# The gate columns leave the front, and a new stage runs the first tile's merge and experts beside the other tiles' gates

## What is computed

```python
h = rmsnorm(x, norm1_w)
z = h @ w_in                       # columns: q, k, v (512 each), forget logits (8), GLU (1024), mq (512), gates (3072)
a = glu[:, :512] * sigmoid(glu[:, 512:])
gates = sigmoid(z[:, OFF_G:]).reshape(n, 3, 1024)
o_fox  = fox_attention(q, k, v, logf) @ w_fox_o
o_conv = silu(layernorm(causal_depthwise_conv31(a))) @ w_conv_o
o_mem  = memory_attention(mq, mk, mv) @ w_mem_o
x = x + (gates[0] * o_fox + gates[1] * o_conv + gates[2] * o_mem) @ w_out
h2 = rmsnorm(x, norm2_w)
# PEER: 8 heads; each picks 16 of 16384 experts for every row
q = (h2 @ w_q).reshape(n, 8, 2, 128)
s1, s2 = q[:, :, 0] @ keys1.T, q[:, :, 1] @ keys2.T        # 128 scores a side
top 16 of each side, top 16 of their 256 sums -> idx, g = softmax(top)
x = x + sum_k g[k] * gelu(h2 . u[idx[k]]) * v[idx[k]]      # u, v: 16384 rows of 1024
```

## Time and profile before

| | us |
|---|---|
| median of 3 runs | 4037.64 (4036.03 to 4041.02) |
| the profiled execution, from its first to its last instruction | 4041.3 |
| front, up to the barrier | 723 |
| attention, up to the barrier | 222 |
| merge of nine tiles | 230 |
| loop of 1088 steps | 2862 |

### The profile page before, as it was taken

How to read it: one execution, slowest core, us unless ns; L and a number is a source line. 1 busy time by engine, 2 the same in 40 slices (tenths; PEclk the granted TensorE clock), 3 DMA queues, 4 the chain that set the end, 5 groups by cost and what they waited for, 6 DMA issues and landing times.

```text
span 4041.3 us, 36528 instructions
## 1 busy us (share of the span) xinstructions
PE 3418.2 (85%) x10586; PEld 1797.4 (44%) x10586; DVE 2646.1 (65%) x6147; ACT 1002.9 (25%) x2536; POOL 2474.0 (61%) x2475
## 2 busy tenths in 40 slices
PE   8999999799988878877877887887888787788787
PEld 6788788455534333333333333333333333333332
DVE  4119944563476777777767777677777777767794
ACT  6111112673222212212222121221222212122131
POOL 4416531232037777777777777777677777777775
PEclk9989999899999999999999999999999999999999
DMA  4402234644279999999999999999999999999998
GB/s 154 129 27 91 99 101 135 168 124 166 84 279 409 409 409 410 409 409 409 402 404 410 407 399 409 405 401 409 405 400 409 408 397 406 409 389 399 409 406 313
DMA packets 419459, 1294.72 MB, mean 320 GB/s; under 512 B 62122, under 2 KB 98246, under 8 KB 419263
## 3 DMA queue, kind: packets, MB, share of 16 engines
q0 software_dynamic: 313344, 1140.99, 71.3%
q1 hardware_dynamic: 104554, 146.81, 11.5%
q10 hardware_dynamic: 1365, 4.60, 0.4%
HBM read 1247.62 MB, written 44.60 MB: 320 GB/s over the span
## 4 chain that ended last, share of the span: by engine, by line
DMA 34%; POOL 22%; PE 12%; issue 8%; DVE 1%; ACT 0%; SPq 0%; DVEq 0%; POOLq 0%
DMA late_v_rows<-in_peer_v,late_expert_idx 23%; POOL late_v_rows L1446 11%; POOL late_u_rows L1438 11%; DMA late_u_rows<-in_peer_u,late_expert_idx 8%; PE late_sums_ps L1635 5%; PE late_sums_ps L1486 4%; DMA late_u_rows<-in_peer_u,late_twin_idx 2%; PE late_q_ps L1526 1%; DMA late_v_rows<-in_peer_v,late_twin_idx 1%; DVE late_u_rows L1916 1%; PE late_h_T_ps L1508 1%; DMA late_w_q_high<-in_peer_w_q 1%; DMA gates<-scr_gates 0%; DMA scr_m<-merged 0%; PE late_rows_ps L1466 0%
## 5 line engine op out<-in xcount | busy, mean ns | idle before, releaser
L1635 PE MATMUL late_sums_ps<-late_v_rows,late_diag 128*128 128x512 f32 (+1 forms) x3840 | 1919.8, 629 | 545.3 <-DMA late_v_rows<-in_peer_v,late_expert_idx 503.5
L1916 DVE CUSTOM_DVE_ANT_0 late_u_rows<-late_u_rows,late_rows_ps 128x1024 f32<-128x1024 f32 x1072 | 1306.5, 1219 | 788.7 <-DMA late_u_rows<-in_peer_u,late_expert_idx 751.8
L1635 PEld LDWEIGHTS late_sums_ps<-late_v_rows,late_diag 128*128 128x128 f32 (+1 forms) x3840 | 682.3, 193 | 1644.3 <-issue 1591.8
L1446 POOL DMA_INDIRECT late_v_rows<-in_peer_v,late_expert_idx x1024 | 992.8, 970 | 404.2 <-issue 248.7
L1438 POOL DMA_INDIRECT late_u_rows<-in_peer_u,late_expert_idx x1008 | 969.6, 962 | 313.2 <-issue 290.5
L1709 ACT ACTIVATE late_gelu<-late_dots 128x4 f32<-128x4 f32 x272 | 55.7, 205 | 2133.1 <-DVE late_dots L1916 2133.1
L457 POOL CAST front_w_upper<-front_w_raw 128x512 fp32r<-128x512 f32 x110 | 107.7, 979 | 332.8 <-DMA front_w_raw<-in_w_in 285.0
L517 PE MATMUL front_products_ps<-front_w_upper,front_x_T_upper 128*128 128x512 f32 x720 | 287.2, 399 | 8.2 <-DVE front_x_T_lower L701 5.3
L1703 ACT ACTIVATE late_diag<-identity,late_weights 128x128 f32<-128x128 f32 x896 | 287.0, 386 | 11.8 <-PE late_sums_ps L1635 8.6
L517 PE MATMUL front_products_ps<-front_w_upper,front_x_T_lower 128*128 128x512 f32 x720 | 282.8, 393 | 0.0
L517 PE MATMUL front_products_ps<-front_w_lower,front_x_T_upper 128*128 128x512 f32 x720 | 282.6, 393 | 0.0
(11 more groups left out here) (251 smaller groups left out, 3666.2 us busy)
## 6 DMA issues: line engine op xcount, KB each, us to landing
front_w_raw<-in_w_in SPq DMA_DIRECT2D x96, 256.0 KB, 5.0
late_v_rows<-in_peer_v,late_expert_idx POOLq DMA_INDIRECT x1024, 15.7
late_u_rows<-in_peer_u,late_expert_idx POOLq DMA_INDIRECT x1008, 15.8
scr_gates<-front_kept_rows SPq DMA_DIRECT2D x48, 256.0 KB, 2.0
gates<-scr_gates SPq DMA_DIRECT2D x24, 512.0 KB, 3.7
front_w_raw<-in_w_mem_kv SPq DMA_DIRECT2D x16, 256.0 KB, 5.6
late_w_out<-in_w_out SPq DMA_DIRECT2D x8, 512.0 KB, 7.2
late_w_q_low<-in_peer_w_q SPq DMA_DIRECT2D x8, 512.0 KB, 13.9
```

Source lines behind the costliest of these rows:

```text
L1446: pool.indirect_dma_start(v[m % V_RING][:], None, io["peer_v"][0], bass.IndirectOffsetOnAxis(ap=rows_of(m), axis=0)).then_inc(s_v[m % V_RI ...
L1635: ins = pe.matmul(acc[0:rows, h, :], diag[k % DIAGS][:, 0:rows], v[n % V_RING][:, h * BANK:(h + 1) * BANK], start=(at == 0), stop=(n == ti ...
L1916: dve.tensor_tensor_reduce(u[n % U_RING][:], u[n % U_RING][:], h2_rows, 1.0, 0.0, ALU.mult, ALU.add, dots[:, n % COLS:n % COLS + 1]).then_ ...
```

## The change

The gates leave the front. `IN_CHUNKS` has eight chunks now. The normalized, turned rows `x` (upper plus lower part, added by GpSimd) are stored in a scratch tensor `xT` of 4.5 MB instead. GLU is made block by block (both halves of one channel block, then the next), so that the convolution can begin after the first block; VectorE's taps are laid between the other work by a plan (`taps_by`: constants for the start and the length of a group and of a tap). From the third chunk on ScalarE makes the upper part of the weights. The gains of q and mq are applied by ScalarE while it copies the turned rows.

A new stage, `opening`, stands between attention and merge. It makes the first tile's gates itself, in full float32 (six groups of eight matmuls), its merge, projection, norm and all eight queries, and routes heads 0 and 1. Then it runs the 128 steps of that tile: VectorE makes the dots and adds seven `v` rows of eight, TensorE one of eight. Beside this TensorE makes the gates of the other eight tiles, 48 groups of eight matmuls in full float32; their weights are loaded again, and the gates are stored in scratch. The place of each group among the steps is fixed by `groups_until`. There are four `u` buffers and three `v` buffers.

`merge_and_experts` then has one tile fewer: eight in the merge, 960 steps in the loop. It loads its first `y` and gates itself, does 32 dots early, and routes three heads behind the merge, four pieces at each half.

```diff
-IN_CHUNKS = ("g0", "mk", "g1", "mv", "ga", "gb", "g2", "g3", "g4", "v", "g5", "q", "k", "mq")
+IN_CHUNKS = ("v", "mk", "mv", "ga", "gb", "q", "k", "mq")
+PE_START, PE_GROUP, PE_SHORT, CONV_START, TAP, TAKE = 113.0, 5.6, 1.6, 143.0, 1.5, 1.9
...
+                        if ci < UPPER_BY_ACT:
+                            pool.wait_ge(s_raw[k], S0 + 16 * (ci + 1))
+                            pool.tensor_copy(wh[b][:, k, :], raw[:, k, :]).then_inc(s_wh, 1)
+                            pool.wait_ge(s_wh, S0 + pool_pieces(ci, k))
+                        else:
+                            pool.wait_ge(s_wu, S0 + KC * (ci - UPPER_BY_ACT) + k + 1)
                         pool.tensor_tensor(wl[b][:, k, :], raw[:, k, :], wh[b][:, k, :].bitcast(F32), ALU.subtract).then_inc(s_wl, 1)
...
+                def taps_by(g):
+                    longs = sum(o.i > first["ga"] and (o.kind not in ("ga", "gb") or o.at < 2) for o in groups[:g.i + 1])
+                    shorts = sum(o.i > first["ga"] and o.kind in ("ga", "gb") and o.at == 2 for o in groups[:g.i + 1])
+                    norms = sum(o.kind == "norm" and o.i > first["ga"] for o in groups[:g.i])
+                    us = PE_START + PE_GROUP * longs + PE_SHORT * shorts - CONV_START - TAKE * norms
+                    return max(0, int(us / TAP))
...
+                    elif g.kind == "norm":
+                        o = groups[g.i - TURN_LAG - 1]
+                        taps_until(taps_by(g))
+                        if g.i == first["q"] + 1:
+                            conv_ends()
+                        take_sums(g)
+                        taps_until(t.taken + 1)
+                        if o.chunk in ("q", "k"):
+                            lower_turned(turn_index[o.i], o.rows, gain_T["q"][:, 0:1] if o.chunk == "q" else None)
+                        take_rows(g)
+                taps_until(CT * CW)
...
-                    if head == HF + 1:
-                        for t in range(2):
-                            sp.dma_start(late.y[t][:], scr["y"].rearrange("j p t -> p j t")[:, :, t * P:(t + 1) * P]).then_inc(late.s_yin[t], 16)
...
-STEPS = NH * TOPK * NT + NH * TOPK // 2
+NE = NT - 1
+STEPS = NH * TOPK * NE + NH * TOPK // 2
-EARLY, EARLY_AT, EARLY_RING = 16, 37, 2
+EARLY, EARLY_AT, EARLY_RING = 32, 17, 2
+ROUTE_AT, ROUTES_EARLY = 12, 3
...
+OPEN_U, OPEN_V, OPEN_DIAGS, KEPT_RING = 4, 3, 4, 2
+OPEN_LAG, OPEN_WEIGHTS = 11, 8
+OPEN_SHARE, OPEN_SHARE_AT = 8, 3
+STEP_US, GROUP_US, GROUPS_LATE_US = 3.05, 7.0, 34.0
+def groups_until(n):
+    return OPEN_GROUPS if n >= OPEN_STEPS + OPEN_LAG else max(0, min(OPEN_GROUPS, int((STEP_US * (n + 1) - GROUPS_LATE_US) / GROUP_US)))
...
+                # opening, GpSimd
+                for n in range(OPEN_STEPS + OPEN_LAG + 1):
+                    if n < OPEN_STEPS:
+                        if n % TOPK == 0:
+                            pool.wait_ge(s_done, S0 + n // TOPK + 1)
+                        if n >= OPEN_U:
+                            pool.wait_ge(s_dot, S0 + n - OPEN_U + 1)
+                        pool.indirect_dma_start(O.u[n % OPEN_U][:], None, io["peer_u"][0], ...)
+                    m = n - OPEN_LAG - 1
+                    if m >= 0:
+                        if m >= OPEN_V and by_tensor(m - OPEN_V):
+                            pool.wait_ge(s_sum, S0 + tensor_rows(m - OPEN_V) + 1)
+                        elif m >= OPEN_V:
+                            pool.wait_ge(s_vsum, S0 + vector_rows(m - OPEN_V) + 1)
+                        pool.indirect_dma_start(O.v[m % OPEN_V][:], None, io["peer_v"][0], ...)
...
+                # opening, TensorE
+                for br in range(3):
+                    gate_logits(2 * br)
+                    gate_logits(2 * br + 1)
+                    ...
+                    product(br)
+                ...
+                for n in range(OPEN_STEPS + OPEN_LAG + 1):
+                    for i in range(done, groups_until(n)):
+                        group(i)
+                    done = max(done, groups_until(n))
+                    if by_tensor(n - OPEN_LAG - 1):
+                        sum_rows(n - OPEN_LAG - 1)
...
+                # opening, VectorE
+                for R in range(2):
+                    for piece in range(TOPK):
+                        route(R, piece)
+                for n in range(OPEN_STEPS + OPEN_LAG):
+                    if n < OPEN_STEPS:
+                        dot(n)
+                    if n % GROUP == 0 and 0 <= n - OPEN_WEIGHTS < OPEN_STEPS:
+                        weights((n - OPEN_WEIGHTS) // GROUP)
+                    m = n - OPEN_LAG
+                    if m >= 0 and not by_tensor(m):
+                        vector_sum(m)
+                    H, j = n // TOPK, n % TOPK
+                    if H + 2 < NH:
+                        route(H + 2, j)
...
+            for r in range(2):
+                load_gates(r)
+                load_y(r)
             L.w_out.load(sp)
...
             attention(nc, io, scr, c, late)
+            opening(nc, io, scr, c, late)
             merge_and_experts(nc, io, scr, c, late, p)
```

974 lines of the change are left out of this document (723 added, 251 removed).

## The result

The changed kernel takes 4017.24 us (median of 4 runs, 4015.02 to 4018.92), the kernel before 4039.31 in the same series: a ratio of 0.994, 95% interval 0.9929 to 0.9952. It is 22 us faster where 108 were forecast, and it lies outside the range (3880 to 4005).

What follows compares the result with a forecast made beforehand. TensorE was taken to bound the front and merge, the DMA engines the main loop; 4041 - 301 (front) - 7 (merge) - 353 (main loop) + 553 (new stage) = 3933, so 3930 us, range 3880 to 4005 with rivals.

Steps and rivals of the forecast that it cites:

- the loop's price by amounts of work: New stage's loop: 128 steps at the DMA sum's 3.15 us a step, 403 us, plus tail 21: 424 us.
- rival (d): New stage: gathers landing later than 7.9 us stall three v buffers, a third of a us a step each; slower; chance 0.09.
- rival (c): New stage's loop: TensorE's sums behind gate groups and slow landings cost 3.6 to 3.9 us a step; 3990 to 4025; chance 0.09.
- The start of the loop: New stage: first dot follows the second routing; TensorE's gate groups start about 36 us on; no stall charged.
- The tail: End of the new stage's loop: 11 vector sums with three v buffers, 1.9 us each, 21 us.
- The head: Start of the new stage, before the first dot: 124 us, bounds 115 to 140.
- The front: Stages before attention: barrier at 422 us instead of 723, 301 less, VectorE's taps last; bounds 405 to 445.
- Rival (b): Front: VectorE's plan does not fit, taps and groups wait for each other, 20 to 45 us more; 3950 to 3975; chance 0.13.
- Attention: Stage after the front: no change, 222 us.
- merge: Stage after the new one: 7 us less, 223 us; bounds 208 to 235.
- main loop: Loop over expert rows after the merge: 353 us less, 2509 us; bounds 2490 to 2530.
- rival (a): New stage's loop runs at VectorE's pace, gate traffic fitting between gathers, 2.9 us a step; about 3890; chance 0.11.

Runs made afterwards that it cites:

- e10: Changed kernel with a fourth v buffer, each v gather issued one step earlier, and one v row added by TensorE instead of 16: 3959.12 us, new stage 563.4.
- e5: Changed kernel with a fourth v buffer and each v gather issued one step earlier: 4214.79 us against 4239.94 for the unaltered one, new stage 588.9.
- e2: Changed kernel with one v row of the new stage added by TensorE instead of 16: 4226.48 us on a slower-gather chip, new stage 593.2.
- e3: Changed kernel with one matmul instead of eight in each of the loop's 48 gate groups: new stage 614.3 us, 3.39 us a step.
- e1: Changed kernel with query copies of heads 4 to 7 inside ScalarE's loop instead of ahead of it: 4251.74 us on a slower-gather chip, new stage 614.5.
- e6: Changed kernel with query copies in ScalarE's loop, one v row by TensorE, gate groups planned 14 us later, three v buffers: 3978.95 us, new stage 578.1.
- e7: Changed kernel with looped query copies, one TensorE v row, groups planned 14 us later, fourth v buffer, earlier v issue: 4189.03 us, 51 less than its control; new stage 561.2.
- e4: Changed kernel reusing two chunks' gate weights and storing one gate row per group in the loop, the other 127 after it: 4691.65 us, 3.30 us a step.
- e8: Changed kernel with one matmul per gate group, two chunks' weights reused, one gate row stored in the loop, all 128 stored after it: 3.11 us a step.

## Why the prediction was wrong

**The step that failed: the loop's price by amounts of work.** The prediction summed TensorE 393, DMA 401 to 416, VectorE 336, and took 3.15 us a step from the upper one. Those sums were about right: e10, with a fourth buffer and one row by TensorE, runs at 3.05, and TensorE's groups took 7.05 us (338.4 us of matmuls for 48) instead of 6.87. (The 409 GB/s that the prediction reads from rows 1 belong to an earlier stretch, 1225 to 1525 us; the row shows 405. No term changes by it.) But the changed kernel does not reach the rates of its engines: the ring of three v buffers turns more slowly. e5 shows that by experiment: 30 us less with the same matmuls and bytes. The life of one v buffer shows where its time goes. Over v gathers 16 to 109 of the changed kernel, for the 82 whose row VectorE adds (93 in e10), means over the trace's instructions:

| us | changed kernel | e10 |
|---|---|---|
| issue until landed | 6.95 | 9.60 |
| landed until its sum starts | 0.15 | 0.25 |
| the sum | 1.28 | 1.28 |
| end of the sum until the next issue into the buffer | 1.79 | 1.19 |
| together | 10.18 | 12.33 |
| divided by the buffers | 3.39 | 3.08 |

The sum of the lines divided by the buffers is the step by construction, in any kernel whose buffers are used in turn; what can be read from it is how the time is divided, and who waits. In the changed kernel 68 of the 82 sums start within 0.1 us of the landing, and VectorE idles 79 us of 322 before them; no dot waits for its u row, which is there 3.3 us early in the mean. In e10 53 of 93 sums start so and VectorE idles 21 us of 287 before them, and the u rows come just in time too (0.4 us before the dot). So e10 is not free of waits for rows; it waits for less, with the DMA engines at 408 GB/s. The twelve rows of TensorE took 12.63 us together (7.24, then 2.85 behind a group, 2.26, 0.27), and with them the v gathers 16 to 112 are 3.49 us apart. The mechanism stood in the prediction as rival (d), and its formula, a third of a us a step for each us, fits; what was mis-sized was the budget, by the time from a sum's end to the next issue. It left "9.5 us less 1.3 for the sum and what the u issue takes" = 7.9 for the landing, 0.3 for GpSimd between the sum and the issue. Measured are 1.79: GpSimd issues u first, each issue 0.94 to 1.99 us, and sits in order behind other waits. That leaves 9.45 - 1.28 - 1.79 - 0.15 = 6.2 at 3.15 us a step, and the landing took 6.95. So the ring bound from a landing of 6.2 us on, not 7.9, and a landing of 6.95 costs 0.24 us a step, the 3.39 of the table. The landing itself was inside the 6 to 9 us that the prediction gave.
The share of the DMA engines misled me before the result and after it. It was 0.97 at 363 GB/s in the changed kernel and 1.03 at 408 in e10: a share near 1 was no full rate. The Trainium skill (Perfetto Trace Analysis, Identifying the Most-Contended Engine) says to judge DMA by HBM utilization, not by occupancy; the two rows agree.

**TensorE's sums behind gate groups, rival (c).** Right in its mechanism; that its time (3990 to 4025) holds the measured 4017 is luck. Its price was 3.6 to 3.9 us a step, and the step was 3.41; the rest of the time came from the start, head and tail, which it did not have. By itself the mechanism is 26 us (e2), and with the fourth buffer 55 (e10), the two nearly adding up. e3 suggests why it could not be mended by a free TensorE alone: there TensorE waits 178.5 us of 250 for rows. That the ring then turns at the pace of the landings is argued; that trace has no landing times.

**The start of the loop.** A term was missing. The prediction had the head end with the second routing, and of the later queries only that TensorE's groups begin some 36 us after the first dot (measured 46). That the second half of the query weights waits for query 3, is whole 24 us after its first issue, and has ScalarE's gelu behind it, was in the change and not in my sum: the second step that failed, put at nothing where it took 20 us. It looks like 27 us in the timeline. What it is worth depends on what stands beside it. Removing it alone gave 4 to 6 us (e1), since the first TensorE row waits for the same thing. With one row by TensorE and three buffers it gave 15 (e6 against e2), and with the fourth buffer 2 (e7 against e10), the last two together with the later plan of the groups. So the hole is real and in none of the three worth the 27 us that it shows. Why it is nearly free with four buffers stays open; in e10 TensorE's 48 groups start at 822.1, after the last query, and TensorE then idles 0.9 us until the last of them ends.

**The tail.** 1.9 us for each of 11 sums was predicted, a term of the sum that was too small by 9 us. Timeline of VectorE in the changed kernel near its end:

```profile
1248.59 1.28 DVE L1895 SCALAR_TENSOR_TENSOR late_x<-open_v_rows,late_weights,late_x 128x1024 f32<-128x1024 f32 x1 [1.36 <-DMA open_v_rows<-in_peer_v,late_expert_idx]
1252.83 1.28 DVE L1895 SCALAR_TENSOR_TENSOR late_x<-open_v_rows,late_weights,late_x 128x1024 f32<-128x1024 f32 x1 [2.96 <-DMA open_v_rows<-in_peer_v,late_expert_idx]
```

A sum of 1.28 and, before ten of the 11, a wait of 0.3 to 3.1 us, nine of them until the row lands: from the end of the last dot at 1226.1 to 1256.3 they take 2.7 each. It is the same ring, now with landings of 4.2 to 5.3 us.

**The head.** 133 against 124, inside its bounds. The first gate group began 14 us into the stage instead of 9, and the output projection took 15.7 us for 13.7; the rest is spread over turns and copies.

**The front.** Right: 427.1 for 422. VectorE's taps are last as predicted (the last ends at 422.4; the mean of 120 of them is 1.42 us for the 1.41 of the sum), and TensorE's last group at 403.5 instead of 391. Rival (b) did not happen.

**Attention, merge, main loop.** Attention took 216.4 us, by the same count of barriers 220.9 before. That is no effect of the change: in the 13 profiles of the changed kernel and its variants, whose attention is the same, it takes 215.1 to 222.0. The merge is 231.0 for 223, inside 208 to 235: without preloads TensorE waits for y until 1268.4. Whether the rest is the routing in seven halves was not tried. The main loop, counted as the prediction counts it, from its first copy at 1493.55 to the end of the last add at 4008.9, is 2515 for 2509, in its bounds.

**The range.** Its lower part hung on rival (a), whose 2.9 us a step no run with gate traffic reached. Its upper end left no room for (c) and (d) together: each was given a time alone, but both act on the same ring, and of the 66 us that the new stage was over, e2 and e5 took back 26 and 30.

## What to carry over

In a loop that streams through small rings, price each ring beside each engine: issue, landing under the load expected, wait in order, use, and the time until the issuer comes round again, divided by the buffers. The largest of engines and rings is the least that the step can be. Where another engine must free a row of the ring, look at what stands before it in that engine's order. A stall in a timeline is worth what the end of the chain gains from its removal, which here was 2 to 15 us for one of 27: two waits stood on the same late load.

## Of the hardware, not expected

Stores of 127 rows were far slower than stores of 128. In e4 the late stores left SBUF as rows 1 to 127; in e8 the same bytes left as rows 0 to 127. The DMA queue of each kernel during those stores (packets, MB, share of 16 engines), first e4 in 420 us, then e8 in 36 us:

```profile
q1 hardware_dynamic: 5676, 11.43, 7.1%
```
```profile
q1 hardware_dynamic: 6672, 12.32, 96.0%
```

27 GB/s against 343, one row of 128 apart (the stores also start one row later). The Trainium skill (DMA: Bandwidth & Descriptors, Why a DMA increments its semaphore by 16 and not by 1) says that the largest number up to 16 that divides the outer dimension of both sides is the number of engines used, one for 127; the share of 7.1%, about a sixteenth, agrees with stores that ran on one engine.

The gathers' rate differs by chip: the main loop with 16 gathers in flight moved 406, 371 and 406 GB/s in the three profiles of the unaltered kernel. On the chip with 371 the new stage of e7, with at most eight in flight, moved 408 GB/s in this stretch:

```profile
1000.00:1100.00 100.00, 100.00 (x233) 41.96 (x232) 90.63 (x170) 36.35 (x46) 71.46 (x65) 1.00 1.03 408
```

It is not the same traffic: gathers were 33.0 of the stretch's 40.8 MB, the rest is gate weights and stores. But the gathers themselves cost less there: their packets took 82.4% of the 16 engines' 100 us, 40 us of one engine a MB, where the same kernel's main loop took 96.0% of 1800 us for 657.0 MB, 42. Why is open; nothing was tried for it.
